# The second block's projections with both halves of x in one 512-column matmul

## The chip, the cores and the metric

The kernel runs on one core of a Trainium2 chip. The metric is the device time of one execution in microseconds (us). TensorE is called PE in the profile, its weight loads PEld, VectorE DVE, ScalarE ACT, GpSimd POOL.

## The reference, cut to what matters

Two blocks follow each other on 256 tokens of width 1024. The first (Hyena, mLSTM, 16 experts) is not touched. The second has two layers, and in each of them `x` goes through wide projections, in float32:

```python
z = jnp.einsum('bsd,dc->bsc', x, w_in) + b_in
q_a, k_a, v_a, q_r, k_r, v_r, g_r, gate_a, gate_b = jnp.split(z, SPLIT_POINTS, axis=-1)
...
y_b = (jax.nn.silu(g_r) * y_r.reshape(B, S, RET_V_WIDTH)).astype(x.dtype)
merged = (jax.nn.sigmoid(gate_a) * jnp.einsum('bsc,cd->bsd', y_a, w_attn_proj)
          + jax.nn.sigmoid(gate_b) * jnp.einsum('bsc,cd->bsd', y_b, w_ret_proj))
...
h = jax.nn.silu(jnp.einsum('bsd,df->bsf', x, w_gate)) * jnp.einsum('bsd,df->bsf', x, w_up)
return jnp.einsum('bsf,fd->bsd', h, w_down)
```

## The kernel before

**Two parts of every number.** In the second block each float32 operand is kept as a high part (rounded to float32r) and a low part (the rest). A product is three matmuls: high by high, high by low, low by high; low by low is dropped (`mm3`). `hTp` holds the parts of x, transposed (8 tiles of 128 channels by 256 tokens), `ybTp` those of the gated retention output (16 tiles), `yaTp`, `mergedp` and `hFp` others.

**Weights.** The weights come in "halves" of 1 MB through a ring of four slots (`half`, SP's queue). A slot is loaded again when the matmuls of the half four places earlier are done. For each half ACT makes the high part (`high_parts`, L901, which runs `AHEAD` = 2 halves in front of the unit that ACT is about to take), then POOL the low part (L715), and PE waits for it (`weights`, `lo_ready`).

**Units.** PE writes its results into eight PSUM banks in a fixed order of "units" (`plan_units`); unit u uses bank u modulo 8, and PE may open it when unit u-8 has been emptied. Each unit is emptied by ACT ("A") or DVE ("V"), counted in `freed_act` and `freed_dve`; `take` waits for a unit, `give` frees it.

**The units of a layer, in order.** `va` (6), `qka` (9), then six rounds of attention, each with scores, `qkr` (3, 3, 2, 0, 0, 0 units), `vr` chunks in the last three rounds, and transposes `pT`; then the retention products `rs` and `ro`, `gate` (8), `gr` with a transposing unit `yrT` behind each (8 of both), `mixA` (4), `mixB` (4), `mixo`, the turned x, `ffgn` and `ffun`, `ffg` and `ffu` in turn (9 of each), `down`. For `qka`, `qkr`, `gate`, `gr`, `ffg` and `ffu` the weights are stationary and x moves, 256 columns (all tokens) at a time: `unit_T` fills one bank with two tiles of 128 output channels, `cols_T` being the loop over the input tiles. `mixB` does the same with `ybTp` and 16 input tiles. In `va`, `vr`, `mixo`, `ffgn`, `ffun` and `down` it is x, or its like, that is stationary and the weights that move, 512 columns at a time (`chunk_N`).

**Emptying.** ACT adds the bias to `qka` (L950) and in place to `qkr` (L967), makes the sigmoid of `gate` (L979) and the silu of `gr` (L989) and `ffg` (L1002). DVE rotates `qkr`, normalizes the retention output (`bn_stats`, L1656, the root by ACT, L1662), multiplies `yrT`, `mixA`, `mixB` and `ffu` by their gates and splits the products into parts. A wait (`link`) stands between DVE's dependent instructions.

Of the kernel before, what the change touches and what calls it, by code (L numbers as in the profile page):

```python
# [26 lines left out]
P = 128  # L27
T = 256
# [43 lines left out]
class Units:  # L72
# [35 lines left out]
def layer_units(units, l):  # L108
# [106 lines left out]
def kernel_program(nc, a, k, out):  # L215
# [3 lines left out]
    with ExitStack() as ctx:  # L219
# [135 lines left out]
        hn = region(19712, 2, 512)  # L355

        hTp = (hT_r[:].rearrange("p (k t) -> p k t", k=KD), parts(26752, KD))
        yaTp = (parts(23936, 3), parts(10752, 3))
        ybTp = (parts(4608, 16), parts(11520, 16))
# [31 lines left out]
        def spread_row(ap, off, n):  # L391
# [37 lines left out]
            lo_ready x_hi out_saved y_ready exp_done x_done rot_biased yr_ready sc_ready  # L429
            soft_arg sg_turned hT_turned aff_exp vb_landed""".split()  # L430
# [92 lines left out]
        for l in range(DEPTH_2):  # L523
# [3 lines left out]
            for i in range(9):  # L527
                add_half(("qka", l), columns(w2, QK_A + 256 * i, 256), U.at(f"qka{l}", i))
            nq = nv = 0
            for j in range(HPG):  # L530
                for i in range(QKR_AT[j]):
                    add_half(("qkr", l, j), columns(w2, QK_R + 256 * nq, 256), U.at(f"qkr{l}.{j}", i))
# [4 lines left out]
            for i in range(8):  # L537
                add_half(("gate", l), columns(w2, GATE_2 + 256 * i, 256), U.at(f"gate{l}", i))
            for i in range(8):
                add_half(("gr", l), columns(w2, G_R + 256 * i, 256), U.at(f"gr{l}.{i}"))  # L540
            for i in range(2):
                add_half(("mixA", l), columns(a["w_attn_proj_2"][l], 512 * i, 512), U.at(f"mixA{l}", 2 * i + 1))
            for i in range(8):
                add_half(("mixB", l), columns(a["w_ret_proj_2"][l], P * i, P), U.at(f"mixB{l}", i // 2), i % 2 == 0)
# [4 lines left out]
            for i in range(2, NF // 2):  # L549
                add_half(("ff", l), columns(a["w_ffn_gate_2"][l], 256 * i, 256), U.at(f"ffg{l}.{i}"))  # L550
                add_half(("ff", l), columns(a["w_ffn_up_2"][l], 256 * i, 256), U.at(f"ffu{l}.{i}"))
# [24 lines left out]
        def wait_emptied(eng, name, n=None):  # L576
# [7 lines left out]
            for u in range(i0, i0 + total):  # L584
                last[U.engine[u]] = U.count[u]
# [133 lines left out]
        def _(act):  # L719
# [188 lines left out]

            def take2(name, i=0):

                high_parts(halves_by(name, i) + AHEAD)
                return take(name, i)

# [4 lines left out]
            def high_x(name, t):  # L918

                for i in range(2):  # L920
                    u = U.at(f"{name}.{t}", i)
                    act.wait_ge(s["unit_done"], u + 1)
                    A.copy(hTp[0][:, 4 * i:4 * i + 4, t * P:(t + 1) * P],
# [17 lines left out]
            for l in range(DEPTH_2):  # L941
# [3 lines left out]
                for i in range(9):  # L945
                    b = take2(f"qka{l}", i)
                    for j in range(2):
                        m = 2 * i + j
                        c = l * P + E_QKA + m
                        ins = A.activation(qka[:, m], b[:, j * T:(j + 1) * T], ACT.Identity, bias=colC[:, c:c + 1])  # L950
                    give(ins)
                for j in range(HPG):
# [7 lines left out]
                    for i in range(QKR_AT[j]):  # L960
                        high_parts(halves_by(f"qkr{l}.{j}", i) + AHEAD)
                        u = U.at(f"qkr{l}.{j}", i)
                        act.wait_ge(s["unit_done"], u + 1)
                        for q in range(2):
                            c = l * P + E_QKR + 2 * (sum(QKR_AT[:j]) + i) + q
                            v = bank[u % 8][:, q * T:(q + 1) * T]
                            ins = A.activation(v, v, ACT.Identity, bias=colC[:, c:c + 1])  # L967
                        ins.then_inc(s["rot_biased"], 1)
# [6 lines left out]
                for i in range(8):  # L975
                    b = take2(f"gate{l}", i)
                    for q in range(2):
                        c = l * P + E_GG + 16 + 2 * i + q
                        ins = A.activation(gates2[:, 2 * i + q], b[:, q * T:(q + 1) * T], ACT.Sigmoid, bias=colC[:, c:c + 1])  # L979
                    give(ins)  # L980
                    if i == 3:
                        next_root(8)
                for i in range(8):
                    b = take2(f"gr{l}.{i}")
                    if i >= 2:
                        act.wait_ge(s["freed_dve"], U.count[U.at(f"yrT{l}.{i - 2}")])
                    for q in range(2):
                        c = l * P + E_GG + 2 * i + q
                        ins = A.activation(gtmp[:, i % 2, q * T:(q + 1) * T], b[:, q * T:(q + 1) * T], ACT.Silu, bias=colC[:, c:c + 1])  # L989
                    give(ins)  # L990
# [5 lines left out]
                for i in range(2, NF // 2):  # L996
                    b = take2(f"ffg{l}.{i}")
# [4 lines left out]
                    give(A.activation(gtmp[:, i % 2], b[:], ACT.Silu))  # L1002
                high_parts(halves_by(f"down{l}.last") + AHEAD)
# [4 lines left out]
        def _(dve):  # L1008
# [492 lines left out]
            nroot = [4]  # L1501

            def next_root(n):

                nroot[0] += 1
                dve.sem_inc(s["var_ready"], 1)
                inv_root(nroot[0], sm[:, 0:n], sm[:, 8:8 + n], sm[:, 16:16 + n])
# [51 lines left out]
            def low_x(name, t, n0):  # L1559

                for i in range(2):
                    b = take(f"{name}.{t}", i)[:].rearrange("p (k t) -> p k t", k=4)
                    dve.wait_ge(s["x_hi"], n0 + i + 1)
                    hi, lo = (v[:, 4 * i:4 * i + 4, t * P:(t + 1) * P] for v in hTp)
# [7 lines left out]
            def split_product(pair, i, name, other):  # L1572

                b = take(name)
                link(tt(b[:], b[:], other))
                split(pair, i, b)

            for l in range(DEPTH_2):
# [4 lines left out]
                for i in range(3):  # L1583
                    wd = 512 if i < 2 else 128
                    for t in range(2):
                        b = take(f"va{l}", 2 * i + t)
                        give(tt(va[:, t, 512 * i:512 * i + wd], b[:, 0:wd], vbias_a[:, 512 * i:512 * i + wd], ALU.add))
                def attention_out(j):
# [7 lines left out]
                for j in range(HPG):  # L1596
# [20 lines left out]
                    if QKR_AT[j]:  # L1617
                        for i in range(QKR_AT[j]):
                            hh = sum(QKR_AT[:j]) + i
                            b2 = take(f"qkr{l}.{j}", i)[:].rearrange("p (q t) -> p q t", q=2)  # L1620
                            dve.wait_ge(s["rot_biased"], RH * 2 * l + hh + 1)
# [35 lines left out]
                next_root(8)  # L1657
                for h in range(RH):
                    for t in range(2):
                        n = 2 * h + t  # L1660
                        v = yr[:, t, h * 512:(h + 1) * 512]
                        link(V.tensor_scalar(v, v, sm[:, 24 + 2 * n:25 + 2 * n], sm[:, 16 + n:17 + n], ALU.subtract, ALU.mult))  # L1662
                    dve.sem_inc(s["yr_ready"], 1)
                for c in range(8):
                    dve.wait_ge(s["freed_act"], U.count[U.at(f"gr{l}.{c}")])
                    split_product(ybTp, c, f"yrT{l}.{c}", gtmp[:, c % 2])
# [4 lines left out]
                for i in range(4):  # L1671
                    m = merged2[:, 2 * i:2 * i + 2].rearrange("p k t -> p (k t)")
                    b = take(f"mixB{l}", i)
# [13 lines left out]
                for i in range(2):  # L1687
                    split(hFp, i, take(f"hnT{l}", i))
                for i in range(2, NF // 2):
                    dve.wait_ge(s["freed_act"], U.count[U.at(f"ffg{l}.{i}")])  # L1690
                    split_product(hFp, i, f"ffu{l}.{i}", gtmp[:, i % 2])
# [7 lines left out]
        def _(pe):  # L1699
# [387 lines left out]

            def cols_T(o, n, c, xT, nk):
# [318 lines left out]
```

## Time and profile before

| | us |
|---|---|
| median of 3 runs | 2568.59 (2568.52 to 2571.02) |
| the profiled execution | 2571.02 |
| its span, first to last instruction | 2569.2 |
| PE busy in the span | 2225.3 (87%) |
| DVE, ACT, POOL busy | 630.4, 597.8, 859.6 |
| second block, within the span | from about 1377 to the end |

The durations used below come from the one profiled execution. A matmul's duration in the profile is longer than the distance to the next one, since they overlap; for the pace one reads the distances between starts.

### The profile page before, as it was taken

The page shows a single profiled execution, that of the slowest core. Times are in us where ns is not written, and L with a number is a line of the kernel's source. Part 1 is how long each engine was busy: PE and PEld are TensorE (multiplying, and loading weights), DVE is VectorE, ACT ScalarE, POOL GpSimd, SP SyncE. Part 2 cuts the span into 40 slices and gives each one's busy share as a digit, 9 for nine tenths or more (in the row PEclk, how much of TensorE's full clock was granted, in tenths as well). Part 3 has the DMA queues.
Part 4 walks back from the last instruction along what each step waited for, and adds up shares of the span by engine and source line. Part 5 has one row for each costly group of instructions (what it writes and reads, how often), then busy time and mean ns, then how long its engine had stood idle before and what let it go on. Part 6 is the DMA issues. An engine that isn't in the chain of part 4 may idle for free.

```text
span 2569.2 us, 33839 instructions
## 1 busy us (share of the span) xinstructions
PE 2225.3 (87%) x14900; PEld 1657.5 (65%) x14900; DVE 630.4 (25%) x1226; ACT 597.8 (23%) x666; POOL 859.6 (33%) x212
## 2 busy tenths in 40 slices
PE   6999998867776766776766999999999999999998
PEld 2678775323333222222325997998997998998997
DVE  5233433111111111111113043433112042433111
ACT  1211300000000000000002443534333443543432
POOL 1000000000000000000004764777887855677885
PEclk9999997887778777778777999999999999999999
DMA  9456324999999999999996643565655744456653
GB/s 345 122 191 235 112 99 196 392 428 428 429 429 429 429 429 429 429 428 428 428 427 220 222 139 115 164 173 196 204 183 173 249 148 131 132 173 197 191 186 131
DMA packets 236700, 680.08 MB, mean 265 GB/s; under 512 B 8748, under 2 KB 153142, under 8 KB 211313
## 3 DMA queue, kind: packets, MB, share of 16 engines
q1 hardware_dynamic: 233905, 671.54, 69.1%
q0 software_dynamic: 2400, 6.41, 1.0%
q8 instruction: 88, 1.44, 0.2%
q10 hardware_dynamic: 288, 0.53, 0.1%
q14 instruction: 19, 0.16, 0.0%
HBM read 673.85 MB, written 4.59 MB: 264 GB/s over the span
## 4 chain that ended last, share of the span: by engine, by line
PE 67%; DMA 27%; DVE 3%; ACT 1%; issue 1%; POOL 0%; SPq 0%; DVEq 0%; ACTq 0%
PE bank L1714 65%; DMA ring_sb<-w_exp 14%; DMA arena_sb<-w_exp 13%; PE bank L1717 2%; DVE arena_sb L1028 1%; DVE bank L1031 1%; DVE x_sb L1031 0%; POOL ring_parts L715 0%; ACT ring_parts L901 0%; DMA arena_sb<-hy_skip 0%; DVE sm_sb L1518 0%; DMA ring_sb<-w_in 0%; SPq L605 0%; DVE arena_parts L1028 0%; DVE x_sb L1028 0%
## 5 line engine op out<-in xcount | busy, mean ns | idle before, releaser
L715 POOL TENSOR_TENSOR ring_parts<-ring_sb,ring_parts 128x2048 fp32r<-128x2048 f32 x186 | 848.9, 4574 | 1387.1 <-ACT ring_parts L901 1386.8
L1714 PE MATMUL bank<-arena_sb 128*32 128x256 f32 (+8 forms) x3550 | 562.1, 546 | 146.5 <-DMA arena_sb<-w_exp 112.7
L1714 PE MATMUL bank<-hT_parts,ring_parts 128*128 128x256 f32 x3264 | 596.3, 285 | 0.0
L1714 PE MATMUL bank<-arena_parts,ring_parts 128*128 128x256 f32 x2544 | 573.2, 284 | 0.0
L1714 PEld LDWEIGHTS bank<-arena_sb 128*32 128x32 f32 (+4 forms) x3550 | 318.1, 182 | 354.0 <-DMA arena_sb<-w_exp 151.9
L1714 PEld LDWEIGHTS bank<-hT_parts,ring_parts 128*128 128x128 f32 x3264 | 511.6, 192 | 1.4 <-issue 1.3
L1714 PEld LDWEIGHTS bank<-arena_parts,ring_parts 128*128 128x128 f32 x2544 | 422.8, 192 | 0.6 <-issue 0.5
L1714 PE MATMUL bank<-ring_sb,arena_sb 128*32 128x512 f32 (+2 forms) x2336 | 302.4, 607 | 136.1 <-DMA ring_sb<-w_exp 136.1
L901 ACT CAST ring_parts<-ring_sb 128x2048 fp32r<-128x2048 f32 x186 | 349.9, 1887 | 276.8 <-DMA ring_sb<-w_ffn_gate 71.2
L1028 DVE TENSOR_TENSOR arena_sb<-bank,arena_sb 128x512 f32<-128x512 f32 (+4 forms) x209 | 129.9, 644 | 771.1 <-PE bank L1714 685.9
L1714 PEld LDWEIGHTS bank<-ring_sb,arena_sb 128*32 128x32 f32 (+1 forms) x2336 | 88.9, 126 | 341.8 <-DMA ring_sb<-w_exp 217.4
L1714 PE MATMUL bank<-ring_parts,arena_parts 128*128 128x512 f32 (+1 forms) x1008 | 274.1, 387 | 0.0
L1714 PEld LDWEIGHTS bank<-ring_parts,arena_parts 128*128 128x128 f32 x1008 | 189.3, 188 | 38.0
L1714 PE MATMUL bank<-ring_parts,hT_parts 128*128 128x512 f32 (+1 forms) x576 | 171.2, 382 | 9.0 <-DVE arena_parts L1028 5.4
L891 ACT COPY arena_sb<-bank 128x256 f32<-128x256 f32 x16 | 6.0, 372 | 594.1 <-PE bank L1714 594.1
L1714 PE MATMUL bank<-hT_sb,ring_sb 128*128 128x256 f32 x640 | 144.2, 387 | 0.0
L1714 PEld LDWEIGHTS bank<-hT_sb,ring_sb 128*128 128x128 f32 x640 | 123.9, 194 | 20.5 <-issue 3.5
L1714 PEld LDWEIGHTS bank<-ring_parts,hT_parts 128*128 128x128 f32 x576 | 105.6, 190 | 30.3 <-DVE arena_parts L1028 6.2
L1028 DVE TENSOR_TENSOR bank<-bank,arena_sb 128x512 f32<-128x512 f32 x66 | 46.0, 697 | 306.7 <-PE bank L1714 230.4
L1717 PEld LDWEIGHTS bank<-ident_sb,arena_sb 128*128 128x128 f32 x426 | 52.8, 160 | 47.3 <-issue 22.5
L1717 PE MATMUL bank<-ident_sb,arena_sb 128*128 128x128 f32 x426 | 66.7, 296 | 18.3 <-DVE arena_sb L1028 6.9
L710 POOL DMA_DIRECT2D arena_sb<-const_ltmask x1 | 0.6, 560 | 236.5 <-PE bank L1717 236.5
(211 smaller groups left out, 953.7 us busy)
## 6 DMA issues: line engine op xcount, KB each, us to landing
arena_sb<-w_exp SPq DMA_DIRECT2D x96, 2048.0 KB, 35.6
ring_sb<-w_exp SPq DMA_DIRECT2D x96, 2048.0 KB, 35.6
ring_sb<-w_in SPq DMA_DIRECT2D x112, 1024.0 KB, 5.4
ring_sb<-w_ada SPq DMA_DIRECT2D x24, 1024.0 KB, 12.2
ring_sb<-w_ffn_gate SPq DMA_DIRECT2D x22, 1024.0 KB, 5.3
ring_sb<-w_ffn_up SPq DMA_DIRECT2D x22, 1024.0 KB, 5.3
ring_sb<-w_ffn_down SPq DMA_DIRECT2D x22, 1024.0 KB, 4.8
ring_sb<-w_ret_proj SPq DMA_DIRECT2D x16, 1024.0 KB, 5.9
```

The lines of the kernel that those rows point to most:

```text
L710: g.dma_start(dst, src).then_inc(s["moe_landed"], 16)
L715: g.tensor_tensor(low, half(n)[0], high.bitcast(F32), ALU.subtract).then_inc(s["lo_ready"], 1)
L891: A.copy(ysb, bank[0][:, 0:T]).then_inc(s["y_evac"], 1)
L901: A.copy(half(n, ring_r)[1], half(n)[0]).then_inc(s["hi_ready"], 1)
L1028: return V.tensor_tensor(o, i0, i1, op)
L1031: return V.scalar_tensor_tensor(o, i0, sc, i1, op0, op1)
L1714: return M.matmul(o, l, r, start=first, stop=last)
L1717: return M.transpose(o, i, ident[:])
```

## The change

The parts of x are laid side by side in memory: for each input tile 256 columns of the high part, then 256 of the low part, so that both can be one moving operand of 512 columns. For each stationary tile of a weight's high part one matmul of 512 columns takes the place of two of 256; the result of (weight high, x low) then lies in the right half of the bank, apart from the rest. The third product, weight low by x high, stays a matmul of 256 columns. A bank now holds one tile of 128 output channels instead of two, so these units double in number. They are emptied in two steps: ACT copies the right half into one of three places of `spare` in SBUF, adding the bias where there is one (`set_aside`), and DVE adds the left half to it (`fold`), writing to SBUF for `qka` and otherwise into the first bank of the pair; for `gate`, `gr` and `ffg` ACT then applies its function to the pair of 512 columns. `mixB` and `ffu`, which DVE took alone before, go through ACT as well. In the gate stage DVE's normalization is cut into eight steps, one after each `fold`, and ACT's square root for it moves from behind gate 3 to behind gate 0. The weight loads, their order and the units in which weights move are as before.

```diff
+    def add_pairs(self, name, n):
+
+        self.add(name, 2 * n, "V")
+        for i in range(n):
+            u = self.at(name, 2 * i)
+            self.count[u], self.count[u + 1] = self.count[u + 1], self.count[u]
...
-    units.add(f"qka{l}", 9, "A")
+    units.add(f"qka{l}", 18, "V")
...
-            units.add(f"qkr{l}.{j}", QKR_AT[j], "V")
+            units.add_pairs(f"qkr{l}.{j}", QKR_AT[j])
...
-    units.add(f"gate{l}", 8, "A")
+    units.add(f"gate{l}", 16, "AV")
     for c in range(8):
-        units.add(f"gr{l}.{c}", 1, "A")
+        units.add(f"gr{l}.{c}", 2, "AV")
...
-    units.add(f"mixB{l}", 4, "V")
+    units.add_pairs(f"mixB{l}", 4)
...
-        units.add(f"ffg{l}.{c}", 1, "A")
+        units.add(f"ffg{l}.{c}", 2, "AV")
...
-        units.add(f"ffu{l}.{c}", 1, "V")
+        units.add_pairs(f"ffu{l}.{c}", 1)
...
+            def set_aside(name, i, c=None):
+
+                high_parts(halves_by(name, 2 * i + 1) + AHEAD)
+                for j in range(2):
+                    u, n = U.at(name, 2 * i + j), folds[0]
+                    folds[0] += 1
+                    act.wait_ge(s["unit_done"], u + 1)
+                    if n >= 3:
+                        act.wait_ge(s["folded"], n - 2)
+                    A.activation(spare[:, n % 3], bank[u % 8][:, T:2 * T], ACT.Identity,
+                                 bias=0.0 if c is None else colC[:, c + j:c + j + 1]).then_inc(s["spared"], 1)
+
+            def take_folded(name, i=0, c=None):
+
+                set_aside(name, i, c)
+                u = U.at(name, 2 * i)
+                assert U.engine[u] == "A", name
+                act.wait_ge(s["folded"], folds[0])
+                return bank[u % 8]
...
                 for i in range(8):
-                    b = take2(f"gate{l}", i)
-                    for q in range(2):
-                        c = l * P + E_GG + 16 + 2 * i + q
-                        ins = A.activation(gates2[:, 2 * i + q], b[:, q * T:(q + 1) * T], ACT.Sigmoid, bias=colC[:, c:c + 1])
-                    give(ins)
-                    if i == 3:
+                    b = take_folded(f"gate{l}", i, l * P + E_GG + 16 + 2 * i)
+                    give(A.activation(gates2[:, 2 * i:2 * i + 2].rearrange("p q t -> p (q t)"), b[:], ACT.Sigmoid))
+                    if i == 0:
                         next_root(8)
...
+            def fold(name, i, outs=None):
+
+                b = bank[U.at(name, 2 * i) % 8]
+                for j in range(2):
+                    n, v = folds[0], bank[U.at(name, 2 * i + j) % 8]
+                    folds[0] += 1
+                    dve.wait_ge(s["spared"], n + 1)
+                    dst = outs[:, j] if outs is not None else b[:, j * T:(j + 1) * T]
+                    tt(dst, v[:, 0:T], spare[:, n % 3], ALU.add).then_inc(s["folded"], 1)
+                dve.wait_ge(s["folded"], folds[0])
+                return b
...
+                for n in range(8):
+                    fold(f"gate{l}", n)
+                    dve.sem_inc(s["freed_dve"], 1)
+                    if n == 0:
+                        inv_root(root8, sm[:, 0:8], sm[:, 8:16], sm[:, 16:24])
+                    h, t = divmod(n, 2)
+                    v = yr[:, t, h * 512:(h + 1) * 512]
+                    link(V.tensor_scalar(v, v, sm[:, 24 + 2 * n:25 + 2 * n], sm[:, 16 + n:17 + n], ALU.subtract, ALU.mult))
+                    if t == 1:
+                        dve.sem_inc(s["yr_ready"], 1)
                 for c in range(8):
+                    fold(f"gr{l}.{c}", 0)
+                    dve.sem_inc(s["freed_dve"], 1)
                     dve.wait_ge(s["freed_act"], U.count[U.at(f"gr{l}.{c}")])
...
+            def wide_T(name, i, n, c, pair, nk):
+
+                w, b = weights(n), open_unit(name, i)
+                for q in range(nk):
+                    v = pair[2 * q // nk][:, q % (nk // 2)]
+                    if q:
+                        mm(b[:, 0:T], w[1][:, q, c:c + P], v[:, 0], False, False)
+                    ins = mm(b[:], w[0][:, q, c:c + P], v.rearrange("p s t -> p (s t)"), q == 0, q == nk - 1)
+                    if q == 0:
+                        mm(b[:, 0:T], w[1][:, q, c:c + P], v[:, 0], False, False)
+                close(ins)
+
+            def unit_wide(name, i, n):
+
+                for j in range(2):
+                    wide_T(name, 2 * i + j, n, j * P, hTp, KD)
...
                 for i in range(9):
-                    unit_T(f"qka{l}", i, half_at["qka", l] + i, hTp)
+                    unit_wide(f"qka{l}", i, half_at["qka", l] + i)
```

## Rows read from the trace of the kernel before

**Rows 1.** Page: the span, busy time by engine, PE's granted clock in 40 slices.

```profile
span 2569.2 us, 33839 instructions
PE 2225.3 (87%) x14900; PEld 1657.5 (65%) x14900; DVE 630.4 (25%) x1226; ACT 597.8 (23%) x666; POOL 859.6 (33%) x212
...
PEclk9999997887778777778777999999999999999999
```

**Rows 2.** Windows: us, busy PE, PEld, DVE, ACT, POOL (x count), PEclk, DMA, GB/s.

```profile
1611.00:1657.00 46.00, 46.00 (x385) 46.00 (x385) 18.65 (x10) 25.13 (x28) 37.09 (x9) 1.00 0.61 184
...
1813.00:1908.00 95.00, 95.00 (x794) 95.00 (x793) 18.44 (x27) 35.38 (x25) 74.75 (x17) 1.00 0.63 202
```

**Rows 3.** The chain that ended last, layer 0: start, duration, what.

```profile
1463.20 0.85 ACT arena_sb L950 x2
...
1657.42 0.44 PE bank L1717 x4
1657.85 5.75 PE bank L1714 x48
...
1701.16 71.07 PE bank L1714 x528
```

**Rows 4.** Costliest groups: the matmuls of 256 columns with parts.

```profile
L1714 PE MATMUL bank<-hT_parts,ring_parts 128*128 128x256 f32 x3264 | 596.3, 285 | 0.0
L1714 PE MATMUL bank<-arena_parts,ring_parts 128*128 128x256 f32 x2544 | 573.2, 284 | 0.0
```

**Rows 5.** DVE's timeline: its first instruction behind two successive ffu units.

```profile
1829.85 0.70 DVE L1028 TENSOR_TENSOR bank<-bank,arena_sb 128x512 f32<-128x512 f32 x1 [9.37 <-PE bank L1714]
...
1841.37 0.70 DVE L1028 TENSOR_TENSOR bank<-bank,arena_sb 128x512 f32<-128x512 f32 x1 [9.37 <-PE bank L1714]
```

**Rows 6.** PE's timeline: in va (128 columns) and in vr (512 columns).

```profile
1406.31 0.28 PE L1714 MATMUL bank<-ring_parts,arena_parts 128*128 128x128 f32 x1
...
1410.66 0.28 PE L1714 MATMUL bank<-ring_parts,arena_parts 128*128 128x128 f32 x1
...
1558.26 0.39 PE L1714 MATMUL bank<-ring_parts,arena_parts 128*128 128x512 f32 x1
...
1567.78 0.39 PE L1714 MATMUL bank<-ring_parts,arena_parts 128*128 128x512 f32 x1
```

**Rows 7.** Groups by shape from 1330 us on: busy, mean ns, idle before.

```profile
L715 POOL TENSOR_TENSOR ring_parts<-ring_sb,ring_parts 128x2048 fp32r<-128x2048 f32 x180 | 830.2, 4622 | 1379.4 <-ACT ring_parts L901 1379.1
...
L901 ACT CAST ring_parts<-ring_sb 128x2048 fp32r<-128x2048 f32 x180 | 341.9, 1906 | 267.6 <-DMA ring_sb<-w_ffn_gate 71.2 <-DMA ring_sb<-w_ffn_down 67.1 <-DMA ring_sb<-w_in 50.1
...
L950 ACT ACTIVATE arena_sb<-bank,colC_sb 128x256 f32<-128x256 f32 x36 | 15.1, 472 | 50.1 <-PE bank L1714 50.1
...
L1002 ACT ACTIVATE arena_sb<-bank 128x512 f32<-128x512 f32 x18 | 10.7, 597 | 77.8 <-PE bank L1714 77.8
...
L1028 DVE TENSOR_TENSOR arena_sb<-bank,arena_sb 128x256 f32<-128x256 f32 x16 | 6.7, 417 | 0.0
```

**Rows 8.** ACT's timeline in the gate stage: behind gate 0, and the root.

```profile
1611.38 0.84 ACT L979 ACTIVATE arena_sb<-bank,colC_sb 128x256 f32<-128x256 f32 x2 [2.06 <-PE bank L1714]
...
1629.51 1.28 ACT L741 ACT_TABLE_LOAD   x1
1630.81 0.21 ACT L741 ACTIVATE sm_sb<-sm_sb 128x8 f32<-128x8 f32 x1
```

**Rows 9.** DVE's timeline in the gate and gr stages.

```profile
1608.51 4.24 DVE L1656 TENSOR_SCALAR sm_sb<-sm_sb 128x8 f32<-128x8 f32 x1
...
1658.33 0.70 DVE L1028 TENSOR_TENSOR bank<-bank,arena_sb 128x512 f32<-128x512 f32 x1 [9.72 <-ACT arena_sb L989]
```

**Rows 10.** POOL's timeline: what it ran at the times of rows 9.

```profile
1608.09 4.62 POOL L715 TENSOR_TENSOR ring_parts<-ring_sb,ring_parts 128x2048 fp32r<-128x2048 f32 x1 [20.67 <-ACT ring_parts L901]
...
1654.41 4.62 POOL L715 TENSOR_TENSOR ring_parts<-ring_sb,ring_parts 128x2048 fp32r<-128x2048 f32 x1 [1.14 <-ACT ring_parts L901]
```

**Rows 11.** DMA issues: count, KB each, median us from issue to landing.

```profile
ring_sb<-w_in SPq DMA_DIRECT2D x112, 1024.0 KB, 5.4
```

More of the change, by code:

```diff
@@ L945, in _ @@
                 for i in range(9):
[L946 to L950, printed above, removed]
-                    give(ins)
+                    set_aside(f"qka{l}", i, l * P + E_QKA + 2 * i)
                 for j in range(HPG):
@@ L960, in _ @@
                     for i in range(QKR_AT[j]):
[L961 to L968 removed]
+                        set_aside(f"qkr{l}.{j}", i, l * P + E_QKR + 2 * (sum(QKR_AT[:j]) + i))
                     for i in range(3):
@@ L1563, in low_x @@
                     dve.wait_ge(s["x_hi"], n0 + i + 1)
-                    hi, lo = (v[:, 4 * i:4 * i + 4, t * P:(t + 1) * P] for v in hTp)
+                    hi, lo = (hTp[i][:, :, s_, t * P:(t + 1) * P] for s_ in range(2))
                     give(tt(lo, b, hi.bitcast(F32), ALU.subtract))
@@ L1570, in split, with fold_first @@
                 give(tt(flat(pair[1], i), b[:], flat(pair[0], i).bitcast(F32), ALU.subtract))
[L1572 to L1576, printed above, removed]
+            def fold(name, i, outs=None):
[8 more added lines that the diff above has]
+                return b
+            def fold_first(name, i):
+                b = fold(name, i)
+                dve.sem_inc(s["freed_dve"], 1)
+                return b
             for l in range(DEPTH_2):
@@ L1587, in _ @@
                         give(tt(va[:, t, 512 * i:512 * i + wd], b[:, 0:wd], vbias_a[:, 512 * i:512 * i + wd], ALU.add))
+                for i in range(9):
+                    fold(f"qka{l}", i, qka[:, 2 * i:2 * i + 2])
+                    dve.sem_inc(s["freed_dve"], 2)
                 def attention_out(j):
@@ L1686, in _ @@
                     give(tt(hn[:, t], b[:], gtmp[:, t]))
-                for i in range(2):
-                    split(hFp, i, take(f"hnT{l}", i))
                 for i in range(2, NF // 2):
+                    fold(f"ffg{l}.{i}", 0)
+                    dve.sem_inc(s["freed_dve"], 1)
+                    if i == 2:
+                        for c in range(2):
+                            split(hFp, c, take(f"hnT{l}", c))
+                    b = fold_first(f"ffu{l}.{i}", 0)
                     dve.wait_ge(s["freed_act"], U.count[U.at(f"ffg{l}.{i}")])
-                    split_product(hFp, i, f"ffu{l}.{i}", gtmp[:, i % 2])
+                    link(tt(b[:], b[:], gtmp[:, i % 2]))
+                    split(hFp, i, b)
                 inner = l < DEPTH_2 - 1
@@ L2121, in first_chunk_N @@
                             w = weights(n + q // 4)
-                        ins = mm3(b[:], both(hTp, slice(None), q, slice(t * P, (t + 1) * P)), both(w, slice(None), q % 4),
-                                  q == 0, q == KD - 1)
+                        ins = mm3(b[:], tokens(q, t), both(w, slice(None), q % 4), q == 0, q == KD - 1)
                         if t == 1 and q == 3:
@@ L2139, in chunk_N @@
                             kt_ = h * nk + q
-                            ins = mm3(banks[t][:, 0:width], both(xT, slice(None), kt_, slice(t * P, (t + 1) * P)),
+                            x_ = tokens(kt_, t) if xT is hTp else both(xT, slice(None), kt_, slice(t * P, (t + 1) * P))
+                            ins = mm3(banks[t][:, 0:width], x_,
                                       both(w, slice(None), q, slice(0, width)), kt_ == 0, kt_ == KD - 1)
@@ L2191, in _ @@
                     for i in range(QKR_AT[j]):
-                        unit_T(f"qkr{l}.{j}", i, half_at["qkr", l, j] + i, hTp)
+                        unit_wide(f"qkr{l}.{j}", i, half_at["qkr", l, j] + i)
                     for i in range(VR_AT[j]):
@@ L2268, in _ @@
                 for i in range(2, NF // 2):
-                    unit_T(f"ffg{l}.{i}", 0, half_at["ff", l] + 2 * (i - 2), hTp)
+                    unit_wide(f"ffg{l}.{i}", 0, half_at["ff", l] + 2 * (i - 2))
                     if i == 2:
@@ L2277, in _ @@
                             close(ins)
-                    unit_T(f"ffu{l}.{i}", 0, half_at["ff", l] + 2 * (i - 2) + 1, hTp)
+                    unit_wide(f"ffu{l}.{i}", 0, half_at["ff", l] + 2 * (i - 2) + 1)
                 banks = [open_unit(f"down{l}", i) for i in range(3)] + [open_unit(f"down{l}.last")]
```

92 lines of the change are left out of this document (45 added, 47 removed).

## The prediction

> **What bounds the kernel now.** I read the page's head first [rows 1]. PE is busy for 87% of the span, and its granted clock is 9 tenths or more in every slice of the second half, where the edit is; "busy" is no proof of pace, so the windows come next. In the gate stage and in the ffg/ffu stage PE is busy without a gap, at a granted clock of 1.00 (the 2.4 GHz level), while DVE is busy 40% and 19%, ACT 55% and 37%, POOL 81% and 79% of the time [rows 2]. The chain of waits says the same in order of time: one piece of 71.07 us with 528 matmuls, or 5.75 us with 48, with 0.44 us of transposes between, and nearly nothing of another engine inside these stages [rows 3]. So in the stages that change, time is PE's issue of matmuls, and the question is what one matmul costs.
>
> Its duration (285 ns [rows 4]) does not tell, since matmuls overlap. The pace does. DVE starts behind each ffu unit at 1829.85 and 1841.37; between lie 96 matmuls of 256 columns, so 11.52 us / 96 = 120.0 ns each [rows 5]. In a vr chunk 14 groups of three 512-column matmuls lie between 1558.26 and 1567.78, so 9.52 / 42 = 226.7 ns each; in va 13 groups of three 128-column ones take 4.35 us, 111.5 ns each [rows 6]. At 2.4 GHz 256 columns are 106.7 ns and 512 are 213.3 ns: both widths pay the columns and 13.3 ns more. At 128 columns the fixed part is 58 ns: there something other than columns, the weight load probably, is the floor of about 111 ns. Both widths that the change uses stay above that floor.
>
> **The matmuls.** Per layer unit_T makes 9+8+8+8+9+9 = 51 units with hTp, each of 2 x 8 triples of matmuls: 816; mixB has 4 x 2 x 16 = 128. Two layers: 1888 triples, 5664 matmuls, which are all but the 144 of mixA among the 5808 of [rows 4]. A triple goes from 3 x 256 columns to 512 + 256: the same 768 columns, one instruction less. Before 3 x 120.0 = 360.0 ns, after 226.7 + 120.0 = 346.7 ns: 13.3 ns saved, 1888 x 13.3 = 25.2 us. A pair of units (one weight half) takes 16 x 0.3467 = 5.55 us in place of 5.76. No row has the 512-column matmul with x moving and weights stationary, nor the two widths in turn. Bound above: if width 512 gave nothing back (240 ns in place of 226.7) the saving is 0. Bound below: the full 25.2; no row has a fixed cost under 13.3. I take 25.2, because the 512-column rows pay the same 13.3 over their columns as the 256-column ones, although operands are swapped between them. The Trainium skill (TensorE: Matmul & The Clock Gate, Back-to-back issue gap) gives a warm gap of N/2.4 + 2.5 ns, 109 ns at 256 columns; the trace has 120.0, so it disagrees, and by the page's figure the change would be an estimated 1888 x 2.5 = 4.7 us.
>
> **The emptying.** It costs nothing while it stays in the shadow of PE. Per weight half DVE gains two adds of 256 columns, 0.42 us each; ACT's two copies are of the kind of the old bias passes (0.47), and gate and gr gain an activation of 0.60 [rows 7]. There are 118 halves, so DVE gets 118 x 0.84 = 99 us more. Per 5.55 us ACT then has 1.91 (high part) + 0.94 + 0.60 = 3.5, DVE at most 0.84 + 2.1 (its product and split of three instructions of 0.7) = 2.9, POOL 4.62. None reaches 5.55.
>
> **The chain behind a unit** matters more, since ACT makes the next high part only when done. Steady, in gate: end of half n, copy 0.47, add 0.42, hand-overs 0.1, sigmoid 0.60, high part 1.91, low part 4.62 [rows 7]: ready 8.1 us after the end, for half n+3, needed at 2 x 5.55 = 11.1. Cover 3.0 us. The load itself (slot free at the end of half n-1, 5.4 us to land [rows 11]) is there before. The tightest later place is mixB's first half: ready 8.1 us behind gr 7, needed after yrT (0.44) and mixA (72 x 0.12 = 8.64), so 9.1; cover 1.0. Behind mixB's last unit copy, add and four DVE instructions take 0.47 + 0.42 + 2.8 = 3.7 us, under mixo's first half (24 x 0.2267 = 5.44).
>
> **Where cover is gone.** First, gate 0, which starts 5.76 before 1611.35, at 1605.6 [rows 8]. DVE's L1656 (8 elements) runs 4.24 us, from 1608.51 to 1612.75, exactly until POOL's subtraction of 1608.09 + 4.62 ends [rows 9, 10]: it is locked out. Before nobody needed DVE then; now fold(gate 0) stands behind it. Counted from gate 0's start: DVE free 7.15, two adds to 8.0, sigmoid to 8.7, the moved root (table load 1.28, root 0.21 [rows 8]) to 10.2, high part of gate 3 to 12.1, low part to 16.8; gate 3 is wanted at 16.6. Loss 0.2 per layer, 0.4 in all. The next halves recover: gate 4's low part is due at 21.5 against 22.2. The eight L1662 steps will likewise wait for POOL's gaps, but each has from +0.9 to the next fold at about +5.5, and POOL's op ends at +2.6. Second, the end of qka: PE waits for the last unit, 0.85 of ACT before [rows 3], 0.47 + 0.42 + 0.05 after: 0.1 per layer, 0.2. The rotation of qkr ends 3.2 us behind the unit in place of 3.0, when the next scores are not ready yet; nothing.
>
> **Sum.** 25.2 - 0.4 - 0.2 = 24.6 us less. The span goes from 2569.2 to 2544.6; the profiled execution's own 2571.02 (1.8 outside the span) to 2546.4; it was 2.4 over the median, so on the median 2568.6 - 24.6 = 2544.0.
>
> **Rivals.**
>
> A, no gain: the 13.3 ns do not go with the instruction (the wide one costs 240 ns). Against it stands the 226.7 [rows 6]; for it only that those rows have other operands. Time 2568.6 + 0.6 = 2569.2; with the page's 2.5 ns 2564.5, also within 0.2% of before. Together 0.05.
>
> B, slower by POOL against the adds. If DVE's add and POOL's subtraction lock each other out as L1656 was, each half becomes a ring: low part 4.62, two adds 0.84, sigmoid or silu 0.60, high part 1.91, hand-overs 0.3 = 8.3 in place of 5.76. 118 halves x 2.5 = 295 us: 2864. It decides the sign once a half takes 0.05 us more than 5.76. Against it: at 1658.33 a DVE product with one operand in PSUM and one in SBUF, the kind of the new adds, took 0.70 us while POOL ran its 4.62 from 1654.41 [rows 9, 10]. Chance 0.04. The Trainium skill (SBUF — State Buffer, Who interferes with whom) says that a DVE instruction with at most one SBUF input outside the two-port modes does not contend with GpSimd, while tensor_scalar can; the trace agrees on both, with 0.70 and 4.24 us.
>
> C, part of the gain given back: in gate, or at mixB, the chain uses up its 3.0 or 1.0 us of cover, because L1662 is caught by two POOL operations in a row or a load is late. One low part late by 0.5 to 1 us at each of the 16 gate halves costs 8 to 16 us: 2552 to 2560. For it: 4.24 us for 8 elements, and the 0.2 above. Against: the cover. Chance 0.10.
>
> **How the numbers follow.** Forecast case 0.78, 2541.5 to 2547; C 0.10; A 0.05; B 0.04; 0.03 for a larger gain (PE's waits elsewhere shrinking). A measurement of this kernel tells a change from none from about 0.2% on, 5.1 us. Faster 0.78 + 0.10 + 0.03 = 0.91, same 0.05, slower 0.04. The range is 2541 to 2552, the forecast case and the near edge of C; what lies outside is most of C, with A and B, under 0.2.
>
> **What the profile after would show.** PE x14900 less 1888, and groups of 1888 matmuls with 512 columns and x moving; 11.09 us between DVE's instructions behind successive ffu units; gr pieces of 5.55 us in the chain; DVE's busy time up 99 us; POOL's subtraction still 4.62; idle time of PE behind L715 up by some tenths at gate 3. Wrong would be: a triple at 0.36 (A), adds over 1 us or POOL over 5 (B), PE idle behind ring_parts L715 for more than 2 us in all in gate or mixB (C).

## The result

| | before | after |
|---|---|---|
| median of 4 runs each, us | 2568.56 (2566.36 to 2571.02) | 2553.71 (2551.32 to 2556.59) |
| the profiled execution | 2571.02 | 2555.60 |
| its span | 2569.2 | 2553.8 |

The kernel became faster by 14.9 us: ratio 0.994, 95% interval 0.9929 to 0.9952. The forecast was 24.6 us less, 2544.0, with a range of 2541 to 2552; the measured time lies 9.7 us above the one and 1.7 above the edge of the other. The direction is as forecast, the size is six tenths of it.

The page's head of the kernel after, for [rows 1]:

```profile
span 2553.8 us, 30814 instructions
## 1 busy us (share of the span) xinstructions
PE 2209.2 (87%) x13012; PEld 1553.4 (61%) x13012; DVE 725.6 (28%) x1446; ACT 648.6 (25%) x786; POOL 859.1 (34%) x212
PEclk9999997787777878778787999999999999999999
```

14900 - 13012 = 1888 matmuls are gone, as counted. DVE is busy 95 us longer, of 99 forecast; POOL is unchanged. The groups of the second block by shape, for [rows 4, 7]:

```profile
L725 POOL TENSOR_TENSOR ring_parts<-ring_sb,ring_parts 128x2048 fp32r<-128x2048 f32 x180 | 829.6, 4626 | 1367.6 <-ACT ring_parts L911 1367.2
L1759 PE MATMUL bank<-arena_parts,ring_parts 128*128 128x512 f32 x1072 | 383.8, 396 | 0.0
L1759 PE MATMUL bank<-hT_parts,ring_parts 128*128 128x512 f32 x816 | 308.6, 401 | 0.3 <-POOL ring_parts L725 0.3
L1046 DVE TENSOR_TENSOR bank<-bank,arena_sb 128x256 f32<-128x256 f32 x184 | 78.7, 432 | 307.0 <-ACT arena_sb L935 304.3
```

The wide matmuls are 1072 + 816 = 1888. An add of `fold` takes 432 ns, and POOL's subtraction 4626 (before 4622): they run side by side without touching. Then the pace, by DVE's timeline of the ffg/ffu stage, as in [rows 5]:

```profile
1822.46 1.28 DVE L1046 TENSOR_TENSOR bank<-bank,arena_sb 128x256 f32<-128x256 f32 x2 [2.00 <-ACT arena_sb L935]
...
1833.65 1.28 DVE L1046 TENSOR_TENSOR bank<-bank,arena_sb 128x256 f32<-128x256 f32 x2 [1.99 <-ACT arena_sb L935]
...
1844.83 1.28 DVE L1046 TENSOR_TENSOR bank<-bank,arena_sb 128x256 f32<-128x256 f32 x2 [1.99 <-ACT arena_sb L935]
```

Two halves, which are 32 triples, take 11.19 us: before 11.52, forecast 11.09. A pair of wide and narrow is 349.7 ns, not 346.7. PE has no gap in this stage, and its granted clock is 1.00, as the windows of the gate and the ffg/ffu stage show, for [rows 2] (columns: stretch, its length, busy time of PE, PEld, DVE, ACT and POOL with their instructions, granted clock, DMA share, GB/s). The first row is a place ahead of the gate stage, to which I come below:

```profile
1585.00:1587.00 2.00, 2.00 (x7) 1.62 (x7) 1.87 (x4) 0.00 (x0) 0.00 (x0) 0.50 0.00 0
1607.00:1652.00 45.00, 44.97 (x258) 38.93 (x257) 26.77 (x27) 29.85 (x36) 36.47 (x9) 1.00 0.61 187
1807.00:1900.00 93.00, 93.00 (x534) 81.03 (x533) 31.98 (x59) 46.02 (x58) 75.45 (x17) 1.00 0.64 207
```

The chain of waits, for [rows 3] (start us, us, what):

```profile
1479.96 0.48 ACT arena_sb L935
1480.47 0.44 DVE bank L1046
1481.05 0.69 DVE arena_sb L1046
1481.74 0.62 DVE bank L1046
1482.38 0.77 DVE arena_sb L1046 x2
1483.14 0.14 issue
1483.28 19.05 PE bank L1759 x114
...
1585.12 33.30 PE bank L1759 x152
1618.46 33.83 PE bank L1759 x192
1652.29 0.44 PE bank L1762 x4
1652.73 5.60 PE bank L1759 x32
...
1694.98 70.14 PE bank L1759 x400
```

There are two things in it that the chain of before did not have. A gr piece is 5.60 us (5.75 before, 5.55 forecast). And behind a qkr pair there now stands a series of six instructions of ACT and DVE, copy, add and rotation, for which PE waits at 1483.28; it comes back at 1502.35 and 1519.15.

### The profile page after: what moved, and what is told of

Its sections match the earlier page's. It is cut to its first block, busy times and chain, and to the rows that moved or that the text cites. A ratio compares the mean times of both kernels' runs of the same rounds, so it can differ in the third digit from the quotient of the medians.

```text
span 2553.8 us, 30814 instructions
## 1 busy us (share of the span) xinstructions
PE 2209.2 (87%) x13012; PEld 1553.4 (61%) x13012; DVE 725.6 (28%) x1446; ACT 648.6 (25%) x786; POOL 859.1 (34%) x212
## 4 chain that ended last, share of the span: by engine, by line
PE 64%; DMA 29%; DVE 4%; ACT 1%; issue 1%; POOL 1%; SPq 0%; DVEq 0%; ACTq 0%
PE bank L1759 63%; DMA arena_sb<-w_exp 24%; DMA ring_sb<-w_exp 4%; PE bank L1762 2%; DVE arena_sb L1046 1%; DVE bank L1049 1%; POOL ring_parts L725 1%; DVE x_sb L1049 0%; DMA arena_sb<-hy_skip 0%; ACT ring_parts L911 0%; DVE sm_sb L1530 0%; DVE bank L1046 0%; ACT arena_sb L935 0%; SPq L615 0%; DVE arena_sb L1049 0%
## 5 line engine op out<-in xcount | busy, mean ns | idle before, releaser
L1759 PE MATMUL bank<-arena_parts,ring_parts 128*128 128x256 f32 (+1 forms) x2288 | 425.9, 334 | 0.0
L911 ACT CAST ring_parts<-ring_sb 128x2048 fp32r<-128x2048 f32 x186 | 349.7, 1886 | 191.4 <-DMA ring_sb<-w_in 61.2
L1759 PEld LDWEIGHTS bank<-arena_parts,ring_parts 128*128 128x128 f32 x2288 | 359.3, 188 | 48.4
L1046 DVE TENSOR_TENSOR arena_sb<-bank,arena_sb 128x512 f32<-128x512 f32 (+5 forms) x245 | 145.1, 611 | 797.0 <-PE bank L1759 689.4
L1759 PE MATMUL bank<-hT_parts,ring_parts 128*128 128x256 f32 (+1 forms) x1632 | 323.0, 340 | 0.3 <-POOL ring_parts L725 0.3
L1759 PEld LDWEIGHTS bank<-hT_parts,ring_parts 128*128 128x128 f32 x1632 | 262.1, 189 | 38.6 <-issue 1.9
L1759 PEld LDWEIGHTS bank<-ring_parts,arena_parts 128*128 128x128 f32 x1152 | 212.7, 188 | 42.7
L1046 DVE TENSOR_TENSOR bank<-bank,arena_sb 128x256 f32<-128x256 f32 (+1 forms) x250 | 124.7, 502 | 323.7 <-ACT arena_sb L935 304.3
L1759 PE MATMUL bank<-ring_parts,hT_parts 128*128 128x512 f32 (+1 forms) x432 | 101.6, 390 | 8.6 <-DVE hT_parts L1046 5.1
L1759 PEld LDWEIGHTS bank<-ring_parts,hT_parts 128*128 128x128 f32 x432 | 79.8, 195 | 26.3 <-DVE hT_parts L1046 5.9
L935 ACT ACTIVATE arena_sb<-bank,colC_sb 128x256 f32<-128x256 f32 x132 | 61.9, 473 | 133.5 <-PE bank L1759 133.4
```

Of the source, the lines that this page charges most:

```text
L911: A.copy(half(n, ring_r)[1], half(n)[0]).then_inc(s["hi_ready"], 1)
L935: A.activation(spare[:, n % 3], bank[u % 8][:, T:2 * T], ACT.Identity, bias=0.0 if c is None else colC[:, c + j:c + j + 1]).then_inc(s["sp ...
L1046: return V.tensor_tensor(o, i0, i1, op)
L1759: return M.matmul(o, l, r, start=first, stop=last)
```

## The experiments

The first four kernels of the table ran on one chip, the other three on another, each group with runs of the kernel before beside it. Ratios are to those.

| kernel | median us (lowest to highest) | ratio, 95% |
|---|---|---|
| after, again | 2555.19 (2551.12 to 2557.33) | 0.9942 (0.9926 to 0.9959) |
| grouped | 2554.65 (2551.27 to 2557.01) | 0.9942 (0.9926 to 0.9959) |
| zigzag | 2552.01 (2547.76 to 2555.22) | 0.9939 (0.9923 to 0.9956) |
| narrow, in the new layout | 2571.06 (2566.83 to 2575.43) | 1.001 (1.0001 to 1.002) |
| before, again | 2568.18 (2566.03 to 2570.87) | 1.0004 (0.9994 to 1.0014) |
| tuned | 2549.14 (2543.91 to 2550.28) | 0.9918 (0.9903 to 0.9933) |
| tuned, with fillers | 2547.69 (2545.78 to 2551.19) | 0.9917 (0.9901 to 0.9934) |

**After, again.** No edit.

> The changed kernel once more, for a second profile. Theories for the 9.2 us by which the profiled gain (15.4) missed 24.6: P (pace): a 512-column matmul and a 256-column one in turn cost 349.6 ns a pair and not 346.7, and mixB's 352.9; this must repeat: units of 2.78 and 2.82 us in turn, 5.647 us for mixB. C (clock): the granted clock fell to 0.5 for 3.41 us in four places of the second block, against one in the kernel before; if that is a property of the change, this profile shows the same places (first scores, yaT of both layers, ffgn of layer 1); if it is chance of where the stretches fall, the places or their number differ, and the time with them by 1.5 us each. Time 2551 to 2557.

It repeats: 2555.19, and the banks are of the same lengths as in the first trace, 2777 and 2817 ns in turn.

**Grouped.** Per bank first one wide matmul, then the eight narrow ones, then the other wide ones: two changes of width in a bank in place of fourteen.

```diff
+                wide(0)
                 for q in range(nk):
-                    if q:
-                        mm(b[:, 0:T], w[1][:, q, c:c + P], v[:, 0], False, False)
-                    ins = mm(b[:], w[0][:, q, c:c + P], v.rearrange("p s t -> p (s t)"), q == 0, q == nk - 1)
-                    if q == 0:
-                        mm(b[:, 0:T], w[1][:, q, c:c + P], v[:, 0], False, False)
+                    mm(b[:, 0:T], w[1][:, q, c:c + P], x_(q)[:, 0], False, False)
+                for q in range(1, nk):
+                    ins = wide(q)
```

> Only PE's order inside a unit is changed: one 512-column matmul, then all 256-column ones, then the other 512-column ones, so that the width changes twice in a unit and not after nearly every matmul. P, in the form that changing width costs: a unit takes 8 x 0.3467 = 2.773 us each time, mixB 5.547, so 204 units x 0.0235 + 16 x 0.10 = 6.4 us less than the changed kernel, about 2547. Rival, that x as the moving operand or the first half of the bank being written again sets the cost: units stay at 2.78 and 2.82, time 2553.

**Zigzag.** The order within a pair turns around from pair to pair (wide, narrow, narrow, wide), so that eight changes are left in a bank.

```diff
-                    if q:
+                    if q % 2:
                         mm(b[:, 0:T], w[1][:, q, c:c + P], v[:, 0], False, False)
                     ins = mm(b[:], w[0][:, q, c:c + P], v.rearrange("p s t -> p (s t)"), q == 0, q == nk - 1)
-                    if q == 0:
+                    if q % 2 == 0:
                         mm(b[:, 0:T], w[1][:, q, c:c + P], v[:, 0], False, False)
```

> Order wide, narrow, narrow, wide, so that the width changes after every second matmul, about 8 times in a unit in place of 15. If each change of width costs, half of the 6.4 us comes back: units of about 2.78 to 2.80, time about 2550. If the cost hangs on something else in the sequence (which of two neighbours is wide at a unit's end), units are all of one length, 2.773 or 2.817.

**Narrow, in the new layout.** Banks, emptying, `spare` and everything else of the kernel after, but three matmuls of 256 columns for each triple, as before.

```diff
-                    ins = mm(b[:], w[0][:, q, c:c + P], v.rearrange("p s t -> p (s t)"), q == 0, q == nk - 1)
...
+                for s_ in range(2):
+                    for q in range(nk):
+                        v = pair[2 * q // nk][:, q % (nk // 2), s_]
+                        ins = mm(b[:, s_ * T:(s_ + 1) * T], w[0][:, q, c:c + P], v, q == 0, s_ == 1 and q == nk - 1)
+                        if s_ == 0:
+                            ins = mm(b[:, 0:T], w[1][:, q, c:c + P], v, False, q == nk - 1)
```

> Layout, banks, spare copies and folds as in the changed kernel, but each 512-column matmul is two of 256 columns: three matmuls of 256 per weight tile, as before the change. This is the emptying alone. If it costs little, as predicted (0.6 us), a unit takes 24 x 0.12 = 2.88 us and the time is that of the kernel before plus 0.6 to 3 us: 2569 to 2572. If the handshake between ACT and DVE were what ate the gain, it would show here as 5 us or more over before: 2574 and up.

The period of DVE's instructions in the ffg/ffu stage, first in grouped, then in zigzag, then in the narrow kernel:

```profile
1824.45 1.28 DVE L1046 TENSOR_TENSOR bank<-bank,arena_sb 128x256 f32<-128x256 f32 x2 [1.98 <-ACT arena_sb L935]
...
1835.62 1.28 DVE L1046 TENSOR_TENSOR bank<-bank,arena_sb 128x256 f32<-128x256 f32 x2 [1.98 <-ACT arena_sb L935]
```

```profile
1830.17 1.28 DVE L1046 TENSOR_TENSOR bank<-bank,arena_sb 128x256 f32<-128x256 f32 x2 [1.97 <-ACT arena_sb L935]
...
1841.32 1.28 DVE L1046 TENSOR_TENSOR bank<-bank,arena_sb 128x256 f32<-128x256 f32 x2 [1.97 <-ACT arena_sb L935]
```

```profile
1828.03 1.28 DVE L1046 TENSOR_TENSOR bank<-bank,arena_sb 128x256 f32<-128x256 f32 x2 [2.15 <-ACT arena_sb L935]
...
1839.55 1.28 DVE L1046 TENSOR_TENSOR bank<-bank,arena_sb 128x256 f32<-128x256 f32 x2 [2.15 <-ACT arena_sb L935]
```

So 11.17, 11.15 and 11.52 us. The last is the period of before to the hundredth: the new layout and the new emptying cost nothing in this stage, and the whole gain comes from the wide matmul. The distances between the starts of successive matmuls, in ns, one bank of ffg or ffu (W 512 columns, N 256), show why the gain is smaller than forecast:

```
narrow    N120 N120 N120 N120 N120 N120 N120 N120 N120 N120 ... (24 of them: 2880)
grouped   W226 N113 N120 N120 N120 N120 N120 N120 N120 W233 W236 W228 W233 W231 W226 W227   (2793)
zigzag    W236 N115 N113 W232 W231 N114 N119 W233 W236 N116 N112 W233 W231 N112 N120 W233   (2786)
after     W235 N116 N113 W232 N118 W231 N112 W233 N117 W231 N112 W233 N117 W231 N113 W232   (2776)
the next  W231 N113 N120 W233 N117 W241 N120 W236 N113 W233 N117 W241 N120 W236 N113 W233   (2817)
```

In grouped a run of wide matmuls settles at 226 to 227 ns and one of narrow ones at 120: these are the two numbers of the forecast, now with x moving. So x as the moving operand is not what costs. But the first wide ones behind a narrow one take 233, 236, 228, 233 and 231, and the first narrow one behind a wide one 113. Eight of each at the settled pace would be 2773 ns. Grouped is 20 above this and zigzag 13; after alternates, bank by bank, between 3 and 44. Neither of the two lengths that were expected for grouped came, 2773 or the pair 2780 and 2820. More changes of width are not simply dearer, since the cheapest bank and the dearest one have the same fourteen.

The medians of after, grouped and zigzag are not apart. By the rows, both new orders save a little: the mean bank of after is 2796.5 ns, so grouped is 3.5 and zigzag 10 below it, and mixB, from its first matmul to the first of mixo, went from 45.17 us to 44.58 and 44.60. In all zigzag's second block is 2.1 us shorter than that of after, from the end of the last va unit on (1129.26 against 1131.34, both in traces without the half-clock stretches that come below); half of 6.4 was expected.

**Before, again**, as a second trace for comparison:

> The kernel before once more, for a second profile of its granted clock. C, as chance: the number or the places of the half-clock stretches in the second block differ from the first profile's one (at the first scores of layer 0), and each costs about 1.5 us where it lies; C, as a property of the change: again only that one. Stages without such a stretch repeat within 0.05 us. Time 2564 to 2571.

Its median is 2568.18, as the first.

The lengths of stages from here on run from the start of the last matmul ahead of a stage to the start of its own last.

**Tuned.** Zigzag, and two edits more. The two adds of a qkr pair write into its second bank, so that the first is free as soon as they are done, not after the rotation; and the normalization's small constant becomes the bias of ACT's square root, so that DVE's `tensor_scalar` (L1683 of the kernel after, L1656 before) is gone.

```diff
-            units.add_pairs(f"qkr{l}.{j}", QKR_AT[j])
+            units.add(f"qkr{l}.{j}", 2 * QKR_AT[j], "V")
...
+            def fold_second(name, i):
...
+                tt(b1[:, T:2 * T], b1[:, 0:T], spare[:, (n + 1) % 3], ALU.add).then_inc(s["folded"], 1)
+                dve.wait_ge(s["folded"], n + 1)
+                tt(b1[:, 0:T], b0[:, 0:T], spare[:, n % 3], ALU.add).then_inc(s["folded"], 1)
+                dve.wait_ge(s["folded"], n + 2)
+                dve.sem_inc(s["freed_dve"], 1)
...
-                link(V.tensor_scalar(sm[:, 0:8], mvr[:, :, 1], LN_EPS, None, ALU.add))
```

> The order wide, narrow, narrow, wide, and two waits taken away: the two halves of a qkr pair are added into the second bank of the pair, so that its first bank, which attn opens next, is free before the rotation; and DVE's 8-element addition of the epsilon, which POOL locked out for 4 us in front of gate 0's fold, is left to ACT's square root as a bias. If attn's wait of 0.26 us is that bank, six attn stages fall from 2.51 to 2.25 us; if gate 3's wait is the lock-out, the gate stage loses its third of a microsecond and is 44.8 in place of 45.14. Sum against the zigzag kernel: 1.6 + 0.6 = 2.2 us, time about 2550. Rival: the rotation, now finished 0.4 us later, delays the next scores, and attn waits as long as before.

First the gate stage in DVE's timeline, the kernel after:

```profile
1604.62 0.18 DVE L1681 BATCH_NORM_AGGREGATE sm_sb<-sm_sb 128x2 f32<-128x6 f32 x1
1604.83 3.99 DVE L1683 TENSOR_SCALAR sm_sb<-sm_sb 128x8 f32<-128x8 f32 x1
1608.97 0.76 DVE L1046 TENSOR_TENSOR bank<-bank,arena_sb 128x256 f32<-128x256 f32 x2
1611.92 0.20 DVE L1054 RECIPROCAL sm_sb<-sm_sb 128x8 f32<-128x8 f32 x1 [2.19 <-ACT sm_sb L751]
```

and tuned:

```profile
1604.31 0.18 DVE L1696 BATCH_NORM_AGGREGATE sm_sb<-sm_sb 128x2 f32<-128x6 f32 x1
1604.72 0.43 DVE L1048 TENSOR_TENSOR bank<-bank,arena_sb 128x256 f32<-128x256 f32 x1 [0.22 <-ACT arena_sb L935]
1607.50 0.43 DVE L1048 TENSOR_TENSOR bank<-bank,arena_sb 128x256 f32<-128x256 f32 x1 [2.35 <-ACT arena_sb L935]
```

In the first, eight elements hold DVE for 3.99 us, to 1608.82, while POOL's subtraction runs from 1604.19 to 1608.80, and the two adds of gate 0 come together behind them; in the second each add runs as its bank is done. In the chain of after a piece ends at 1618.42 and another begins at 1618.46, where PE waits for gate 3's low part; in that of tuned the same 344 matmuls are one piece:

```profile
1585.64 65.91 PE bank L1773 x344
```

The gate stage is 45.14 us in zigzag and 44.80 in tuned: 0.34 a layer. Then two rows of PE's waits, for the second block of the kernel after (us in total, times, longest):

```profile
PE bank L1759 <- POOL ring_parts L725: 3.8, 3, 1.8
...
PE bank L1759 <- DVE arena_sb L1046: 1.3, 6, 0.2
```

The second is the wait for the rotation, and the first of its six stands in PE's timeline where the chain above comes back to PE:

```profile
1483.28 1.97 PE L1759 MATMUL bank<-arena_sb 128*128 128x64 f32 x16 [0.21 <-DVE arena_sb L1046]
```

The same view of tuned has no such row, and its first three attention products of each layer, six in all, take 2.25 us each, as before; in after, zigzag and the narrow kernel they take 2.51. The rival of the expectation, that the later rotation holds up the next scores, did not come.

**Tuned, with fillers.** To this, per layer 6 and 5 matmuls whose result nobody reads, where PE has little to do around the last attention product.

```diff
+                def warm(b, n):
+
+                    for _ in range(n):
+                        mm(b[:, T:2 * T], hTp[0][:, 0, 0, 0:P], hTp[0][:, 0, 0])
...
+                    if j == HPG - 1:
+                        warm(b, 6)
...
+                warm(open_unit(f"yaT{l}", 0), 5)
```

> As the tuned kernel, and PE fills its two idle gaps of 0.68 and 0.64 us around attn 5 with 6 and 5 matmuls of 256 columns whose results nobody reads. If the half-clock stretch at yaT comes from those gaps, it is gone in both layers (yaT 4.4 and ro 15.4 us, plus up to 0.3 us of fillers that do not fit); cost if it would not have come anyway: 0 to 1 us. Time 2548 to 2551.

From 1390 to 2540 us this trace has no stretch below clock 1.00, while that of tuned has one, in layer 1 at 2367. But that one lies at `ffgn`; at `yaT`, where the fillers stand, tuned had none either, so this run does not tell whether they prevent one. The medians, 2547.69 and 2549.14, are not apart: their intervals lie over each other.

**Four executions for the clock**, after, before, after, before, one of each profiled, on a third chip:

> A third profile of the changed kernel, for its half-clock stretches in the second block (4 and 3 so far, against 1 and 0 in the kernel before). If the change makes them likelier, again 2 or more, with stages otherwise as before to 0.1 us. If it was chance, 0 or 1 now.

> A third profile of the kernel before: 0 or 1 half-clock stretch if the change makes them likelier, 2 to 4 possible if it was chance.

> A fourth profile of the changed kernel: 2 or more half-clock stretches if the change makes them likelier, 0 or 1 if the first two profiles were chance.

> A fourth profile of the kernel before: 0 or 1 half-clock stretch if the change makes them likelier, 2 to 4 possible if it was chance.

Their times are 2558.47, 2567.86, 2549.62 and 2569.52. They are for the first row of the windows above: from 1585 to 1587 the kernel after ran at 0.50, the 1.2 GHz level, in the retention products. In the fastest of the four, the second of the kernel after, this place is at 1.00:

```profile
1583.00:1587.00 4.00, 4.00 (x22) 3.20 (x21) 3.16 (x6) 0.00 (x0) 0.00 (x0) 1.00 0.00 0
```

Such short stretches come at three kinds of place, all at or behind a part in which PE waits or has only few short matmuls: the first scores of a layer with the qkr units behind them, `yaT` with the retention products, and `ffgn`. Counted from 1390 to 2530 us: 4, 3, 2 and 0 in the four profiles of after; 1, 0, 1 and 1 in those of before; 3 in grouped, 2 in the narrow kernel, 1 in tuned, none in zigzag and with the fillers. What one costs is read from the stages: `yaT` 4.92 in place of 4.41 and `rs` with `ro` 16.38 in place of 15.41, together 1.5 us; `ffun` in layer 1 14.57 in place of 12.94, so 1.6.

## Why the prediction was right in direction and wrong in size

The cleanest pair are two traces without such a stretch, that fastest one of the kernel after (span 2547.8) and before, again (2564.2). They are 16.4 us apart, and 16.4 in the second block alone (1131.34 against 1147.78 from the end of the last va unit on). Even by this the median would have come to 2552.2, outside the range. The steps of the sum against it:

| term | forecast | measured |
|---|---|---|
| matmuls | -25.2 | -18.7 |
| gate 3 | +0.4 | +0.7 |
| end of qka | +0.2 | +0.3 |
| bank of the qkr pair | 0 | +1.5 |
| sum | -24.6 | -16.2 (the spans say -16.4) |

**The failed step is the term "The matmuls"**, "I take 25.2". The count of 1888 was exact, and the mechanism is right: an instruction of 256 columns pays 13.3 ns over its columns, and going without one gives this back, as the settled 226.7 and 120 of grouped show with x moving. (With each matmul a weight load went too, PEld x14900 to x13012; no run tells which of the two the 13.3 ns belong to.) Its size was off by a cost between the two widths, of which no row of before could tell, since both widths ran there only among themselves. In ffg/ffu a pair takes 349.7 ns, so 10.3 ns are saved for each of 1632 triples, 16.8 us; in mixB, the chain piece that holds mixA, mixB and the start of mixo went from 71.07 to 70.14, which is 0.93 / 128 = 7.3 ns for each of 256, so 1.9. Together 18.7. I had said that no row has "the two widths in turn" and had bounded the term by 0 and 25.2, and then took the upper end as it stood, from rows in which each width ran by itself. The values between got no chance of their own: the forecast case ended at 2547, and what lay beyond it was rival C, for another reason. Rival A is refuted: a wide matmul costs 227 when it stands among its like and 231 to 236, at times 241, behind a narrow one, which itself then costs 112 to 120. Single pairs reach 361, but on the mean a pair is 349.7 in ffg/ffu and 353 in mixB. By the formula of the Trainium skill (TensorE: Matmul & The Clock Gate, Back-to-back issue gap), N/2.4 + 2.5 ns, an estimate of this term was 4.7 us; the runs have 18.7, so the measurement stands against it, as the 120.0 of [rows 5] did. The same section calls that formula the gap of a single, isolated matmul, which the prediction left out, and for a stream in which each matmul has its weight load gives about 81 ns at 128 columns and 131 at 512. Those figures don't fit this case either: [rows 6] has 111.5 and 226.7.

**The emptying costs nothing** where I said so. The narrow kernel has all of it and runs ffg/ffu, gr and mixB of layer 0 at 104.65, 49.51 and 46.08 us, the times of before. Its median is 1.001 of before, with the waits of attention and the later end of qka in it, 1.8 us by the rows. Rival B is refuted: adds of 432 ns and POOL at 4626, over 184 and 180 instructions. The Trainium skill (SBUF — State Buffer, Who interferes with whom) has a DVE instruction with at most one SBUF input, outside the two-port modes, not contending with GpSimd, and `tensor_scalar` able to. The runs agree with both: the adds, with one operand in PSUM, stayed at 432 ns, and the `tensor_scalar` with its operands in SBUF took 3.99 us in after for 8 elements and up to 3.7 us in the L1694 steps.

**Gate 3** is late by 0.34 a layer, not 0.2, for the reason given: taking L1683 away takes it back. Of rival C that is all that came; its 8 to 16 us did not. The groups above have 0.3 us in all of PE's idle time behind `ring_parts` ahead of the matmuls with x moving, where its sign asked for more than 2; the rest of the 3.8 us in the waits lies ahead of matmuls in which x is stationary.

**The rotation of qkr, "nothing", cost 1.5 us.** The step asked when the next scores are ready, and that was right. It did not ask for the bank: a pair has two now, the first stays taken until the rotation has ended, and the attention product eight units on needs it. It costs 0.26 us at six places, by the 2.51 and 2.25, so 1.5 us. The same holds in the narrow kernel, and tuned has none of it.

**The end of qka** has a copy and an add ahead of the first scores. The first scores, counted from qka's last matmul, take 3.22 us in the narrow kernel and 3.06 before: 0.16 a layer against 0.1.

**The spread of the medians.** From the clean 16.4 there are 1.5 us to the 14.9 of the first medians, and 3.6 to the 12.8 of the repeat (2567.98 less 2555.19). The traces have two sources for such differences. One is the stretches at half clock. From the end of the last va unit on, the four traces of after take 1137.26, 1136.12, 1134.66 and 1131.34 us with 4, 3, 2 and 0 of them, those of before 1149.07, 1147.78, 1148.92 and 1148.96 with 1, 0, 1 and 1. Take 1.5 us off for each, and after lies between 1131.3 and 1131.7 and before between 1147.4 and 1147.8: the change is worth about 16 us in all of them, and on the means of four, with the stretches in, 13.8. The other source is the part ahead, the first block and va, whose matmuls the change leaves alone: it ends between 1407.3 and 1412.9 in the same eight traces. In the first pair of traces 4 against 1 stretches make 4.6 us, which 3.6 us less in that part nearly took back: so its 15.4.

**What stays open.** Whether the change brings such stretches, 2.25 on the mean in four profiles of after against 0.75 in four of before, or the traces met them by chance is not settled: after shows anything from 0 to 4, and the four other kernels with wide matmuls had 3, 1, 0 and 0, the narrow one 2. Nor is it known why a bank of the same sixteen matmuls takes 2776 ns and the next 2817. And one row has no term: `down` of layer 0, which the edit does not touch, is 0.2 to 0.5 us shorter in the traces of after than in those of before.

## What to carry to other kernels

Merging matmuls gives back their fixed cost, here 13.3 ns each, but between two widths the pace must be measured as they alternate: rows of each width by itself gave 25 us where 19 came. When a unit takes two banks instead of one, go through every unit that stands eight banks behind it, not only the one that reads the result. A tiny DVE instruction with all operands in SBUF can stand for 4 us beside POOL; once other work is queued behind it, fold it into a neighbour, as the bias of an activation. And set a difference of a few us between medians beside the stages of the traces before explaining it: here a part that nobody had touched moved by 5.5 us.

The best version is tuned, with or without the fillers: 2549.14 and 2547.69 us, 0.8% under before. The interval of its ratio still touches that of after; by the traces it takes 1128.66 and 1126.91 us from the end of the last va unit on, against 1131.34 of after without a stretch.

## What the runs showed of the hardware that was not expected

The start distance of a matmul depends on the widths around it. Behind a change from 256 to 512 columns it is 233, 236, 228, 233, 231 ns until it settles at 227; behind one from 512 to 256 it is 113 and then 120. In strict alternation with sixteen input tiles it runs in a cycle of 232, 118, 241, 120, 236, 113, on average 353 ns a pair where 346.7 would be the sum of both alone.

And a stretch at 1.2 GHz, of 1.5 us in cost, came and went between executions of one kernel at the same place, while every slice of the second block shows 9 tenths in the page's head: only a view of a few us shows it.
